# Gate and up projections of a SwiGLU in quads of 26 products instead of two units of 7

## The chip, the cores and the metric

One core of a Trainium2 chip runs the whole program. The metric is the device time of one execution in microseconds. The kernel has five instruction queues that matter here: PE (TensorE), DVE (VectorE), ACT (ScalarE), POOL (GpSimd) and SP, which only issues DMAs.

## The reference, cut to what matters

A two-layer decoder step for 512 prompt tokens and 8 x 4 sample tokens, so NT = 544 columns, all in float32. Layer 0 mixes tokens with sparse attention, layer 1 with a Mamba-2 scan; after each mixer comes

```python
x += swiglu(rms_norm(x, g), w_gate, w_up, w_down)

def swiglu(h, w_gate, w_up, w_down):                 # D_MODEL = 1024, FFN_HIDDEN = 2816
    return (jax.nn.silu(h @ w_gate) * (h @ w_up)) @ w_down
```

The change is in `h @ w_gate` and `h @ w_up` of both layers.

## The kernel before, in words

Activations lie transposed: 128 features on the partitions, 544 tokens in columns, cut in two halves n1 and n2 of 272. Every big projection is done by a fast matrix multiplication with 7 instead of 8 block products. A **unit** takes two weight tiles (128 outputs each), splits the inner dimension in two halves and the tokens in two halves, and so has 2x2 blocks of weights and 2x2 blocks of moving data. For gate and up an inner half is KH = 4 tiles of 128, so a product (`product`, L336) is 4 matmuls of 128x128 weights against 272 columns, added up in one PSUM bank. A float32 matmul stands in the trace as two records.

Around the products there are three kinds of sums. POOL forms four sums of weight blocks per unit (`weight_sums`, L391, each 128x512 for gate and up and 128x1408 for down); it may overwrite the sums of two units before only when PE has used them. DVE forms four sums of moving blocks once per stage (`moving_sums`, L407, each 128x1088). DVE and ACT then combine the seven products of a unit: ACT copies products 0 and 2 out of PSUM (`copy_product`, L360), DVE does seven additions of 272 columns (`sum_products`, L367), six of which read PSUM and one only SBUF (L387).

`swiglu` (L2199) runs, per layer, 22 gate and up units (unit 2k holds two gate tiles, unit 2k+1 the two up tiles of the same outputs) and then 4 down units, whose inner half is FH = 11 tiles. A gate or up tile is multiplied by rstd (the norm's factor, which is computed while the first units run) on DVE (L2313, L2316); ACT applies SiLU to the gate tiles (L2282); DVE multiplies gate and up (L2321) into `ffn_act`. When an upper tile of `ffn_act` is there, DVE at once makes its four sums for the down units (`act_turns`, L2294 to L2297).

The order on each queue is written out by hand and every instruction of ACT, DVE and POOL also waits for the one before it on its queue (`InOrder`). In the first gate and up units PE runs the four products that need no sums first (`EARLY`), then the norm's column sums (L497 strips, L505), then the rest. Weights come in slots of 1 MB through a ring of four (`ring_rounds`); SP refills a slot when PE signals `w_used`, for gate and up with the fourth product of every second unit. For the first down unit POOL's sums wait for all moving sums, and PE runs the first four products before it needs more than two of them:

```python
elif v == GU_UNITS and j >= 3:                                   # first down unit
    pe.wait_ge(f_sums, 4 * u + (2 if j == 3 else 4))
```

Of the kernel before, what the change touches and what calls it, by code (L numbers as in the profile page):

```python
# [19 lines left out]
P = 128  # L20
# [145 lines left out]

class InOrder:
# [13 lines left out]
def build(nc, t):  # L181
    ctx = ExitStack()
    with ctx:
# [102 lines left out]
        GU_UNITS, D_UNITS = FT, KT // 2  # L286
        U_NSA_IN, U_NSA_OUT, U_FFN, U_SSD_IN, U_SSD_OUT = 0, 10, (14, 64), 40, 60
        TURNS_BEFORE = {"nsa_in": 0, "nsa_out": 4, "ffn0": 8, "ssd_in": 12 + FH, "ssd_out": 16 + FH, "ffn1": 16 + 4 * KT + FH}
# [3 lines left out]


        unit_at, at = {}, 0
        for u in range(90):
            if u in (U_NSA_OUT, U_SSD_OUT):
# [4 lines left out]
            at += 9 if u in (U_NSA_IN, U_SSD_IN) + U_FFN else 7  # L301
# [3 lines left out]
        EARLY = [(0, 0), (0, 1), (1, 0), (1, 1)] + [(u, j) for u in range(2) for j in range(2, 7)]  # L305
        EARLY_SSD = [(0, 0), (1, 0), (0, 1), (1, 1)] + [(0, j) for j in (4, 6, 3, 5, 2)] + [(1, j) for j in range(2, 7)]
        early_at = {(u0 + u, j): n for u0, order in [(U_SSD_OUT, EARLY_SSD)] + [(u0, EARLY) for u0 in U_FFN]
                    for n, (u, j) in enumerate(order)}

        def pair_of(u):  # L310
            return max(u0 for u0 in (U_SSD_OUT,) + U_FFN if u0 <= u)

        def bank_of(u, j):
            if u < U_NSA_OUT:
                return (7 * u + j) % 6
            if (u, j) in early_at:
# [43 lines left out]
        def copy_product(act, do, u, j, dst):  # L360

            act.wait_ge(f_mm, multiplied(u, j))
            if u:
                act.wait_ge(f_added, 5 * (u - 1) + (2 if j == 0 else 5))
            do(act.activation(dst, bank_in(u, j), ACT.Copy), f_copied)  # L365

        def sum_products(dve, do, u, regs, c0, c1, after_u=None, between=lambda step: None):  # L367
# [4 lines left out]
            dve.wait_ge(f_copied, 2 * u + 1)  # L372
# [13 lines left out]
            dve.wait_ge(f_copied, 2 * u + 2)  # L386
# [182 lines left out]
        def p1_pe(pe):  # L569
# [48 lines left out]
            for u in range(10):  # L618
# [9 lines left out]
                for j, (a, b) in enumerate(operands(pair_slot(s), in_sums_of(u), (b11, b21, b22), in_t)):  # L628
# [13 lines left out]
                    if j >= 3:  # L642
                        pe.wait_ge(f_sums, 4 * u + {3: 2, 4: 2, 5: 3, 6: 4}[j])
# [1479 lines left out]
        def p5_pe(pe):  # L2123
            bank_user.clear()
            b11, _, b21, b22 = four_blocks(qT)
            for i in range(4):
                u, s = U_NSA_OUT + i, slot_at["nsa_out"] + i
                in_slot(pe, s)
                for j, (a, b) in enumerate(operands(pair_slot(s), out_sums[i % 2], (b11, b21, b22), out_t)):
# [4 lines left out]
                    if j >= 3:  # L2134
                        pe.wait_ge(f_sums, 4 * u + {3: 2, 4: 2, 5: 3, 6: 4}[j])
# [1376 lines left out]
```

## Time and profile before

| | us |
|---|---|
| median of 3 runs (lowest to highest) | 2271.1 (2264.6 to 2271.8) |
| span of the profiled execution, which is its own time here | 2268.8 |
| PE busy in it | 2153.3 |
| DVE busy | 1340.2 |
| POOL busy | 801.5 |
| ACT busy | 516.6 |

Times in the rows are microseconds from the span's start unless marked ns. "L346" is a line of the kernel, often a helper's; "sbuf<-sbuf,ps" says that an instruction writes SBUF and reads SBUF and PSUM; "xN" counts instructions (PE: records); "idle ... <-" says how long the engine stood idle before such instructions and what ended that. The chain of waits follows the work that ended last back to what released it. PEclk is the granted clock of TensorE as a share of full speed.

### The profile page before, as it was taken

What the parts mean: (1) busy time and instruction counts of PE and PEld (TensorE: products, weight loads), DVE (VectorE), ACT (ScalarE), POOL (GpSimd) and SP (SyncE); (2) the same over time, 40 slices, a digit from 0 to 9 for tenths busy, and PEclk for the clock granted to TensorE, in tenths of its full rate; (3) what the DMA queues carried; (4) which work ended last, traced back from release to release, by engine and by line L of the source; (5) the groups of instructions that cost most, each with busy time, mean ns of one, the idle gap of its engine ahead of it and who ended that gap; (6) DMA issues with size and microseconds to landing.
All of it is one profiled execution on the core that took longest, in us unless ns stands there. A gap on an engine that the chain in (4) does not pass through costs nothing.

```text
span 2268.8 us, 33739 instructions
## 1 busy us (share of the span) xinstructions
PE 2153.3 (95%) x11958; PEld 1703.1 (75%) x11958; DVE 1340.2 (59%) x2172; ACT 516.6 (23%) x1195; POOL 801.5 (35%) x702
## 2 busy tenths in 40 slices
PE   8999999998897679999999999999998999999999
PEld 6867777887675458888888878888556778888887
DVE  4456878764884125645652258876898445556422
ACT  2112112113685212111100023232563011111000
POOL 3321000001211742534325235554694533434242
PEclk8999999997899789999999999999999999999999
DMA  4134352313112962622112222222241221122212
GB/s 174 66 121 143 112 158 75 103 59 112 63 39 83 331 259 75 223 94 92 75 52 102 76 94 75 77 92 81 95 174 68 112 75 75 75 86 89 77 60 83
DMA packets 87735, 236.59 MB, mean 104 GB/s; under 512 B 11441, under 2 KB 60722, under 8 KB 73234
## 3 DMA queue, kind: packets, MB, share of 16 engines
q1 hardware_dynamic: 66722, 191.97, 23.7%
q0 software_dynamic: 7024, 29.90, 3.9%
q10 hardware_dynamic: 13824, 12.59, 1.8%
q8 instruction: 96, 1.57, 0.3%
q14 instruction: 69, 0.57, 0.1%
HBM read 217.95 MB, written 23.73 MB: 107 GB/s over the span
## 4 chain that ended last, share of the span: by engine, by line
PE 72%; DVE 15%; ACT 3%; issue 3%; SPq 3%; ACTq 1%; DMA 1%; POOL 1%; DVEq 0%; POOLq 0%
PE ps L346 57%; PE ps L1022 3%; PE ps L1538 2%; PE ps L1551 2%; PE ps L1571 1%; SPq L1861 1%; ACTq L862 1%; DVE sbuf L2577 1%; PE ps L935 1%; SPq L862 1%; ACT ps L3001 1%; DVE sbuf L1179 1%; DVE sbuf L1170 1%; DVE sbuf L1178 1%; DVE sbuf L1176 1%
## 5 line engine op out<-in xcount | busy, mean ns | idle before, releaser
L346 PE MATMUL ps<-sbuf 128*128 128x272 f32 x6048 | 1402.0, 394 | 19.2 <-DMA sbuf<-w_nsa_in 8.5
L346 PEld LDWEIGHTS ps<-sbuf 128*128 128x128 f32 x6048 | 1149.4, 191 | 269.5 <-issue 17.2
L396 POOL TENSOR_TENSOR sbuf<-sbuf 128x512 f32<-128x512 f32 (+2 forms) x90 | 135.7, 1508 | 710.1 <-PE ps L346 451.2
L365 ACT ACTIVATE sbuf<-ps 128x272 f32<-128x272 f32 x180 | 71.6, 398 | 1067.9 <-PE ps L346 1039.7
L1022 PE MATMUL ps<-sbuf 128*128 128x256 f32 (+1 forms) x1280 | 297.7, 392 | 5.5 <-ACT sbuf L1100 2.9
L1022 PEld LDWEIGHTS ps<-sbuf 128*128 128x128 f32 x1280 | 243.3, 191 | 58.5 <-issue 8.2
L376 DVE TENSOR_TENSOR sbuf<-sbuf,ps 128x272 f32<-128x272 f32 x90 | 39.4, 438 | 230.7 <-PE ps L346 229.6
L405 POOL TENSOR_TENSOR sbuf<-sbuf 128x512 f32<-128x512 f32 (+2 forms) x90 | 141.9, 1577 | 7.7 <-PE ps L346 0.9
L402 POOL TENSOR_TENSOR sbuf<-sbuf 128x512 f32<-128x512 f32 (+2 forms) x90 | 137.1, 1524 | 12.3 <-DVE sbuf L413 5.3
L397 POOL TENSOR_TENSOR sbuf<-sbuf 128x512 f32<-128x512 f32 (+2 forms) x90 | 134.6, 1496 | 7.1
L384 DVE TENSOR_TENSOR sbuf<-sbuf,ps 128x272 f32<-128x272 f32 x90 | 39.4, 438 | 123.5 <-PE ps L346 122.8
L379 DVE TENSOR_TENSOR sbuf<-sbuf,ps 128x272 f32<-128x272 f32 x90 | 39.3, 437 | 120.1 <-PE ps L346 119.1
L387 DVE TENSOR_TENSOR sbuf<-sbuf 128x272 f32<-128x272 f32 x90 | 103.3, 1148 | 3.1
L373 DVE TENSOR_TENSOR sbuf<-sbuf,ps 128x272 f32<-128x272 f32 x90 | 39.4, 438 | 85.6 <-PE ps L346 69.7
L1779 POOL MEMSET sbuf<- 128x512 f32 x1 | 0.5, 524 | 240.9 <-DVE sbuf L1231 240.9
L2316 DVE TENSOR_TENSOR sbuf<-sbuf 128x544 f32<-128x544 f32 x84 | 79.0, 940 | 2.9
L1726 DVE CUSTOM_DVE_ANT_0 sbuf<-ps,sbuf 128x128 f32<-128x128 f32 (+3 forms) x128 | 56.7, 488 | 32.0 <-PE ps L1538 25.1
L1630 ACT ACTIVATE sbuf<-sbuf 128x128 f32<-128x128 f32 (+3 forms) x128 | 70.6, 559 | 3.4 <-DVE sbuf L1726 3.3
L2577 DVE SCALAR_TENSOR_TENSOR sbuf<-sbuf 128x568 f32<-128x568 f32 x72 | 58.4, 811 | 19.3 <-ACT sbuf L2476 16.9
L389 DVE TENSOR_TENSOR sbuf<-sbuf,ps 128x272 f32<-128x272 f32 x90 | 39.3, 437 | 37.1 <-PE ps L346 34.7
L1861 POOL DMA_DIRECT2D sbuf<-sel_k x64 | 35.3, 552 | 65.3 <-ACTq L249 54.4
L1638 ACT ACTIVATE sbuf<-ps 128x128 f32<-128x128 f32 (+3 forms) x128 | 49.3, 434 | 38.0 <-PE ps L1551 37.2
(374 smaller groups left out, 2254.7 us busy)
## 6 DMA issues: line engine op xcount, KB each, us to landing
sbuf<-w_gu SPq DMA_DIRECT2D x44, 1024.0 KB, 4.9
sbuf<-w_down SPq DMA_DIRECT2D x32, 704.0 KB, 5.5
sbuf<-cmp_pages SPq DMA_DIRECT2D x160, 128.0 KB, 2.4
sbuf<-w_ssd_in SPq DMA_DIRECT2D x20, 1024.0 KB, 4.8
sbuf<-cmp_pages ACTq DMA_DIRECT2D x96, 128.0 KB, 3.1
sbuf<-w_nsa_in SPq DMA_DIRECT2D x9, 1024.0 KB, 4.8
sbuf<-sel_k SPq DMA_DIRECT2D x64, 128.0 KB, 2.5
sbuf<-sel_v SPq DMA_DIRECT2D x64, 128.0 KB, 5.1
```

Source lines behind the costliest of these rows:

```text
L346: last = pe.matmul(ps[:, bank_of(u, j), 0:HALF], a[:, kt * P:(kt + 1) * P], b[:, kt], start=kt == 0, stop=kt == kts - 1)
L365: do(act.activation(dst, bank_in(u, j), ACT.Copy), f_copied)
L387: do(dve.tensor_tensor(c1[:, n1], c1[:, n1], p4, ALU.add))
L396: do(pool.tensor_tensor(sv[:, 0], a21, a22, ALU.add), f_sums)
L397: do(pool.tensor_tensor(sv[:, 1], sv[:, 0], a11, ALU.subtract), f_sums)
L402: do(pool.tensor_tensor(sv[:, 2], a11, a21, ALU.subtract), f_sums)
L405: do(pool.tensor_tensor(sv[:, 3], a12, sv[:, 1], ALU.subtract), f_sums)
L1022: last = pe.matmul(product_of(u, j, ht), w[:, kt * 256 + ht * P:kt * 256 + (ht + 1) * P], moving[:, kt], start=kt == 0, stop=kt == KT - 1)
L1630: act.activation(S_, S_, ACT.Exp, scale=-1.0, bias=low[:, 0, s % 3, x:x + 1], accum_out=low[:, 1, s % 3, x:x + 1]).then_inc(a_exp, 1)
L1861: sp.dma_start(dst[:, i:i + 1], src[bass.ds(page, 1)].rearrange("o p n -> p o n")).then_inc(unit_in[place(kind, b)], 16)
L2316: do(dve.tensor_tensor(c[:, x], c[:, x], rstd, ALU.mult), g_took if v % 2 == 0 else None)
L2577: do(dve.scalar_tensor_tensor(acc[:, x], raw[:, x, k:k + CONV], conv_w[:, c, k:k + 1], acc[:, x], ALU.mult, ALU.add), r_conv if k == 3 els ...
```

## The change

Two units (two gate tiles, two up tiles, that is a gate unit and its up unit) become one **quad**: 4 weight tiles, the inner dimension in 4 quarters of KQ = 2 tiles, 2 token halves. It has 26 block products of 2 matmuls instead of 14 of 4. There are 11 quads a layer; the down units keep their 7 products.

- PE does the 26 products in a written order (`PRODUCTS`). Several products follow each other in one PSUM bank as a *chain*: PE goes on adding where the last product stood, but only when ACT (`COPIED`) or DVE (`SUMMED`) has read the value in between.
- POOL makes 28 sums of weight blocks a quad, each 128x256, in the order in which the products need them. They live in 13 places; a sum waits until the product that used its place is done. By the tables the 3rd sum is needed by the 3rd product, the 13th first by the 9th, the 28th by the last (26th). 15 sums of a layer's first quad find a place before any product; the 16th waits for product 3. POOL no longer waits for DVE's moving sums; it starts on them behind the sums of the output projection before.
- DVE makes 18 moving sums (*turns*) of 128x544 at the start of a layer's quads (11 of them before its first addition) instead of 4 of 128x1088. Per quad it does 19 additions of 272 columns, 15 of which read PSUM, then four products by rstd and, one quad later, two `gated` products, all 544 columns.
- ACT copies 9 values a quad (2 x 2 before) and does the two SiLUs of the quad before ahead of B1's copy.
- The moving sums of the down units are made in few long instructions: `lo` (11 tiles) in the 9th quad, `turn2` over 9 tiles in the 11th, and `turn4`, `turn3` and the last two tiles of each behind the last quad. POOL's sums for the first down unit wait for the last gated product.
- The two weight slots of a quad are released by its last product. out_win's store moves on POOL's queue from the 4th unit to the 2nd quad. ACT waits for two earlier stores, since buffers lie elsewhere.

```diff
+SUMMED = ("G1", "D3", "A1", "C1", "E2", "A2", "B3", "A3", "I1", None, "H2", "B4", "E4", "C3", "G2", "F4", None, None, None)
+        def quad_products(pe, n, block, place, raw, turned, before):
...
+            for i, p in enumerate(PRODUCTS):
+                a, b = FACTORS[p]
+                chain, k = IN_CHAIN[p]
+                bank = quad_banks[l][q][chain]
+                before(i)
...
+                else:
+                    name = chain + str(k)
+                    if name in COPIED:
+                        copied(pe, n, name)
+                    if name in SUMMED:
+                        summed(pe, n, SUMMED.index(name))
+                if isinstance(a, int):
+                    pe.wait_ge(f_sums, 4 * units_before(n) + len(SUMS) * n + SUMS.index(a) + 1)
...
+                for kt in range(KQ):
+                    last = pe.matmul(ps[:, bank, 0:HALF], weights[:, kt * P:(kt + 1) * P], moving[:, kt],
+                                     start=k == 0 and kt == 0, stop=kt == KQ - 1, skip_group_check=k > 0)
+                    if kt == 0 and i == len(PRODUCTS) - 1:
+                        last.then_inc(w_used, 2)
+                last.then_inc(f_mm, 1)
+        def quad_weight_sums(pool, do, n, block, place, waits):
...
+            for i, name in enumerate(SUMS):
+                x, op, y = BLOCK_SUMS[name]
+                if waits[i] > 0:
+                    pool.wait_ge(f_mm, products_before(units_before(n) - 1) + 7 + waits[i])
+                do(pool.tensor_tensor(place[i], place[SUMS.index(x)] if isinstance(x, int) else block(x),
+                                      place[SUMS.index(y)] if isinstance(y, int) else block(y), ops[op]), f_sums)
...
+                        if isinstance(b, int):
+                            pe.wait_ge(f_turns, TURNS_BEFORE[f"gu{l}"] + MOVING_ORDER.index(b) + 1)
+                        else:
+                            norm.wait_scaled(pe, KQ * int(b[0]) + KQ)
+                        if i == 5:
+                            norm.pe_strips(pe)
+                        if i == 8:
+                            norm.pe(pe)
...
+                def before_kt(v, j):
+                    def ready(kt):
+                        if j == 1:
+                            pe.wait_ge(prod, f0 + FH + kt + 1)
+                        elif j == 2 and kt in (0, READY):
+                            pe.wait_ge(f_turns, t0 + (2 if kt == 0 else 5))
...
+                for q in range(FFN_QUADS):
+                    c = quad_c[q % 2]
+                    quad_sums(dve, do, n0 + q, quad_regs, c, between(q))
+                    if q == 0:
+                        norm.invert(dve, do)
+                    for x in GATE_ROWS:
+                        do(dve.tensor_tensor(c[:, x], c[:, x], rstd, ALU.mult), g_took)
+                    for x in range(2):
+                        do(dve.tensor_tensor(c[:, x], c[:, x], rstd, ALU.mult))
+                turn4(slice(0, READY))
+                gated(FFN_QUADS - 1)
+                turn3(slice(0, READY))
+                turn2(LATER)
+                turn4(LATER)
+                turn3(LATER)
...
             def pool_part(pool):
+                if l == 0:
+                    pool.wait_ge(f_mm, multiplied(U_NSA_OUT, 0))
+                for q in range(FFN_QUADS):
+                    in_slot(pool, s0 + 2 * q)
+                    in_slot(pool, s0 + 2 * q + 1)
+                    quad_weight_sums(pool, pool_do, n0 + q, block_of(q), *places(q))
...
-                    if v == GU_UNITS:
-                        pool.wait_ge(f_turns, t0 + 4 + FH)
+                    if v == 0:
+                        pool.wait_ge(prod, f0 + FT)
+                    weight_sums(pool, pool_do, down_weights(v), down_sums, u0 + v - 1 if v else None)
```

## Rows read from the trace of the kernel before

**Rows 1.** The page, busy us of each engine (share of the span) and instructions

```profile
PE 2153.3 (95%) x11958; PEld 1703.1 (75%) x11958; DVE 1340.2 (59%) x2172; ACT 516.6 (23%) x1195; POOL 801.5 (35%) x702
```

**Rows 2.** Chain of waits, whole run: start us, length us, what

```profile
911.46 286.24 PE ps L346 x1248
...
1198.06 121.24 PE ps L346 x528
```

**Rows 3.** Busy by stretch: window, length, PE PEld DVE ACT POOL busy, PEclk, DMA, GB/s

```profile
911.40:1177.40 266.00, 265.94 (x1161) 220.54 (x1162) 157.20 (x244) 32.08 (x64) 102.58 (x80) 1.00 0.31 114
```

**Rows 4.** POOL by line in 911.5:1177: busy us, mean ns | idle before <-releasers

```profile
L397 POOL TENSOR_TENSOR sbuf<-sbuf 128x512 f32<-128x512 f32 x20 | 25.4, 1272 | 1.6
L396 POOL TENSOR_TENSOR sbuf<-sbuf 128x512 f32<-128x512 f32 x19 | 24.0, 1266 | 134.8 <-PE ps L346 126.9 <-DMA sbuf<-w_gu 7.9
```

**Rows 5.** POOL by line and shape, whole run

```profile
L396 POOL TENSOR_TENSOR sbuf<-sbuf 128x1408 f32<-128x1408 f32 x8 | 25.3, 3160 | 163.0 <-DVE sbuf L2297 62.6 <-DMA sbuf<-w_down 62.1 <-PE ps L346 38.3
...
L396 POOL TENSOR_TENSOR sbuf<-sbuf 128x1024 f32<-128x1024 f32 x4 | 9.4, 2354 | 52.2 <-DVE sbuf L3272 23.3 <-PE ps L346 21.7 <-DMA out_ssm_p<-sbuf 7.2
...
L3241 POOL TENSOR_TENSOR sbuf<-sbuf 32x256 f32<-32x256 f32 x4 | 3.2, 804 | 0.3
```

**Rows 6.** Timeline, POOL, 1009 to 1012.5: start us, length us, what

```profile
1009.90 1.27 POOL L402 TENSOR_TENSOR sbuf<-sbuf 128x512 f32<-128x512 f32 x1
1011.24 1.35 POOL L405 TENSOR_TENSOR sbuf<-sbuf 128x512 f32<-128x512 f32 x1
```

**Rows 7.** Timeline, DVE, 1009 to 1012.5

```profile
1009.91 1.55 DVE L387 TENSOR_TENSOR sbuf<-sbuf 128x272 f32<-128x272 f32 x1
```

**Rows 8.** DVE by line and shape, whole run

```profile
L376 DVE TENSOR_TENSOR sbuf<-sbuf,ps 128x272 f32<-128x272 f32 x90 | 39.4, 438 | 230.7 <-PE ps L346 229.6
...
L2321 DVE TENSOR_TENSOR sbuf<-sbuf 128x544 f32<-128x544 f32 x44 | 31.9, 725 | 1.5
...
L470 DVE RECIPROCAL sbuf<-sbuf 128x544 f32<-128x544 f32 x4 | 14.2, 3552 | 0.1
...
L2294 DVE TENSOR_TENSOR sbuf<-sbuf 128x272 f32<-128x272 f32 x22 | 9.7, 442 | 0.8
...
L412 DVE TENSOR_TENSOR sbuf<-sbuf 128x1088 f32<-128x1088 f32 x4 | 5.2, 1292 | 0.1
```

**Rows 9.** Timeline, POOL, 1209 to 1225

```profile
1216.59 3.52 POOL L402 TENSOR_TENSOR sbuf<-sbuf 128x1408 f32<-128x1408 f32 x1
```

**Rows 10.** Timeline, DVE, 1213 to 1225

```profile
1214.00 3.09 DVE L2306 TENSOR_TENSOR sbuf<-sbuf 128x544 f32<-128x544 f32 x1
1217.13 3.29 DVE L465 TENSOR_SCALAR sbuf<-sbuf 128x544 f32<-128x544 f32 x1
```

**Rows 11.** Chain of waits, 885 to 915

```profile
898.04 1.97 PE ps L497 x32
...
902.04 0.92 PE ps L505 x4
902.96 7.35 PE ps L346 x32
...
911.46 3.68 PE ps L346 x15
```

**Rows 12.** Timeline, DVE, 889 to 912

```profile
893.09 0.50 DVE L465 TENSOR_SCALAR sbuf<-sbuf 128x544 f32<-128x544 f32 x1
```

**Rows 13.** ACT by line and shape, whole run

```profile
L365 ACT ACTIVATE sbuf<-ps 128x272 f32<-128x272 f32 x180 | 71.6, 398 | 1067.9 <-PE ps L346 1039.7 <-DVE sbuf L376 16.3 <-DVE sbuf L389 7.9
L2282 ACT ACTIVATE sbuf<-sbuf 128x544 f32<-128x544 f32 x44 | 28.9, 657 | 6.7 <-DVE sbuf L2316 4.8
```

**Rows 14.** The page, DMA issues: count, KB each, median us from issue to landing

```profile
sbuf<-w_gu SPq DMA_DIRECT2D x44, 1024.0 KB, 4.9
sbuf<-w_down SPq DMA_DIRECT2D x32, 704.0 KB, 5.5
```

**Rows 15.** Timeline, POOL, 1180 to 1200

```profile
1194.81 3.15 POOL L405 TENSOR_TENSOR sbuf<-sbuf 128x1408 f32<-128x1408 f32 x1
```

More of the change, by code:

```diff
@@ new lines, with sums_in_order, need @@
+COPIED = ("D1", "H1", "F1", "D2", "F2", "B1", "E1", "B2", "C2")
+SUMMED = ("G1", "D3", "A1", "C1", "E2", "A2", "B3", "A3", "I1", None, "H2", "B4", "E4", "C3", "G2", "F4", None, None, None)
+MOVING_ORDER = (8, 15, 16, 20, 21, 10, 14, 12, 9, 22, 24, 11, 19, 13, 17, 18, 23, 25)
+def sums_in_order():
+    order = []
+    def need(n):
+        if isinstance(n, int) and n not in order:
+            need(BLOCK_SUMS[n][0])
+            need(BLOCK_SUMS[n][2])
+            order.append(n)
+    for p in PRODUCTS:
+        need(FACTORS[p][0])
+    return tuple(order)
@@ new lines, with sum_places @@
+SUMS = sums_in_order()
+PLACES = 13
+def sum_places(quads):
+    taken_by = {n: i for i, p in enumerate(PRODUCTS) for n in [FACTORS[p][0]]}
+    last_sum = {x: i for i, n in enumerate(SUMS) for x in BLOCK_SUMS[n]}
+    free, out = [(0, -1, -1)] * PLACES, []
+    for q in range(quads):
+        for i, n in enumerate(SUMS):
+            at = min((x for x in range(PLACES) if free[x][1] < q * len(SUMS) + i), key=lambda x: free[x][0])
+            out.append((at, free[at][0]))
+            by = len(PRODUCTS) * q + taken_by[n] + 1 if n in taken_by else free[at][0]
+            free[at] = (by, q * len(SUMS) + last_sum.get(n, -1), 0)
+    return out
@@ L2211, in weights @@
[L2211 to L2219 removed]
+            t0 = TURNS_BEFORE[f"down{l}"]
+            n0 = l * FFN_QUADS
@@ new lines, in between, with at_step @@
+                def between(q):
+                    def at_step(step):
+                        if q == 0 and step == 0:
+                            norm.take_strips(act, act_do)
+                        if q == 0 and step == 1:
+                            norm.root(act, act_do)
+                        if q and step == 2:
+                            silus(q - 1)
+                    return at_step
+                for q in range(FFN_QUADS):
+                    quad_copies(act, act_do, n0 + q, quad_regs, between(q))
@@ new lines, in between, with at_step @@
+                def between(q):
+                    def at_step(step):
+                        for name in TURNS_AT.get((q, step), ()):
+                            if name == MOVING_ORDER[15]:
+                                dve.wait_ge(n_ss, whole(norm.i))
+                            quad_turn(dve, do, name, raw, bc)
+                        if q and step == 2:
+                            gated(q - 1)
+                        if q == FFN_QUADS - 3 and step == 2:
+                            do(dve.tensor_tensor(lo[:, :, n2], lo[:, :, n2], lo[:, :, n1], ALU.subtract))
+                        if q == FFN_QUADS - 1 and step == 4:
+                            turn2(slice(0, READY))
+                    return at_step
```

413 lines of the change are left out of this document (260 added, 153 removed), and 16 rows, old and new, of tables (BLOCK_SUMS, FACTORS, TURN_SUMS).

## The prediction

> **What bounds the kernel now.** I read the page first, then the chain of waits, then the busy time of one stretch, then POOL and DVE line by line in it. The page shows PE busy 95% of the span [rows 1], and the chain shows how: in each layer's gate, up and down stage it is one unbroken run of L346 matmuls, 1248 records in 286.24 us and 528 in 121.24 us, which is 0.2294 and 0.2296 us a record [rows 2]. A matmul is two records, so the first kind of run holds products of 8 records and the second products of 22, at the same pace: the start of a product, with its waits, costs PE nothing visible, and halving products should cost nothing there. Between 911.4 and 1177.4 PE is busy 265.94 of 266.00 us, at a granted clock of 1.00, so 2.4 GHz; POOL is busy 102.58 us there [rows 3], and its idle time is almost all spent waiting for PE to free the places of its weight sums, 126.9 of 134.8 us in front of L396 [rows 4]. So PE is the bound and POOL has slack, which the change spends.
>
> **PE: what goes.** Two units are 14 products of 8 records, 112 x 0.2294 = 25.69 us. A quad is 26 products of 4 records, 104 x 0.2294 = 23.86 us. That is 1.83 us a quad, 20.2 us for 11 quads, 40.4 us for two layers.
>
> **POOL: what comes.** A quad needs 28 sums of 128x256 in place of 8 of 128x512. The trace has no 128x256 sum. The nearest rows lie on a line: 1.27 us for 512 columns [rows 4], 2.35 for 1024 and 3.16 for 1408 [rows 5], so 2.11 ns a column and a constant 0.18; that gives 0.72 at 256. Bounds: half of the 512 sum, 0.63, from below, and the 0.80 us of the 32x256 product of L3241 [rows 5] from above; I take the line's 0.72. One sum starts 0.08 us after the end of the one before (1009.90 + 1.27 to 1011.24) [rows 6]. 28 x 0.80 = 22.4 us of a 23.86 us quad, where two units used 8 x 1.35 = 10.8.
>
> On top come DVE instructions that read two operands from SBUF. L387 takes 1.55 us when it meets a POOL sum [rows 7] and the same shape takes 0.44 where POOL is idle [rows 8]: it ends 0.3 us after the sum that it met, and the next sum takes 1.35 instead of 1.27 [rows 6], 0.08 to 0.09 more. After a 544-column one the POOL sum takes 3.52 [rows 9] instead of 3.16: 0.36 more, half of DVE's own 0.725 [rows 8]. Nor do they pass each other: L2306 and L465 each sit out a whole sum, 3.09 and 3.29 us [rows 10]. A quad has four such instructions of 272 columns (three ends of sums and n35 + F2) and six of 544 (four by rstd, two gated), so POOL loses 4 x 0.09 + 6 x 0.36 = 2.5 us: 24.9 us a quad. DVE itself has room: 15 PSUM reads at 0.44 plus ten instructions that each wait for at most one sum come to some 17 us.
>
> The Trainium skill ("SBUF — State Buffer", section "Who interferes with whom") says that VectorE and GpSimd share a pair of SBUF ports under an exclusive lock, and that the loser stays blocked for the whole instruction of the winner. On the waiting side the rows agree (3.09 us); on POOL's side they show half the instruction, 0.36 of 0.725. By the rule POOL would lose 4 x 0.44 + 6 x 0.725 = 6.1 us a quad, and a quad would take 28.5 us; by the rows 24.9. I take the rows.
>
> So POOL, not PE, sets the pace in the long run, by 24.9 - 23.86 = 1.05 us a quad. It starts ahead: 15 sums find a place before the first product, while PE is still in the output projection. The tight spot is the 9th product, which is first to need the 13th sum. After product 3 POOL works freely through sums 16 to 28 (13 x 0.89, that is 24.9 / 28 each, to 14.3 us into quad 1) and the first 13 of quad 2 (to 25.9 us); the 9th product of quad 2 comes at 23.86 + 8 x 0.917 = 31.2: 5.3 us ahead. Quad 1 changes that little: PE also does the norm's 2.9 us [rows 11] and some stalls, and POOL meets 18 turns at 0.36. I take 4 us of lead, gone after four quads; the last six run at POOL's pace: 6 x 1.05 = **+6.3 us** a layer.
>
> Two long DVE turns hold POOL up for longer: 11 tiles (2992 columns) in quad 9 and 9 tiles (2448) in quad 11. On the line of 0.44, 0.725 and 1.29 us [rows 8] they take 3.27 and 2.71 us; POOL loses all but 0.36 of each: **+5.2 us** (bounds: 1, if POOL has slack then and only PE's wait for DVE is left, and 6.0).
>
> **The start.** Before, PE ran its four early products, strips (1.97 us), norm (0.92) and lost 1.15 us between 902.96 + 7.35 and 911.46 [rows 11]. Now the first three products need six scaled tiles; the 4th needs the eighth, at 893.59 [rows 12], about when it comes. The 6th needs the second turn, at 0.76 us a turn alone or 1.16 behind sums, so 0.8 us late; the 22nd needs the 17th turn, 0.6 us late: **+0.3 us** net (bounds -1 and 3). ACT's two new waits are for stores that are over: POOL waited for out_ssm_p ahead of its first output-projection sum [rows 5], and the first copy comes behind a whole product after that. The store of out_win leaves POOL's queue about a quad later; nothing on the path reads it.
>
> **Quad 2.** DVE finishes quad 1 (4.3 us), inverts (3.55 [rows 8]) and scales two gate tiles (2.3); then ACT, in order, does two SiLUs (0.66 each) ahead of B1's copy (0.40) [rows 13]: at about 12.6 us with hand-overs, for a product due at 13 x 0.917 = 11.9: **+1.0 us** (0 to 2). In later quads the invert is gone and the copy is in time by some 0.5 us. Weights, now released by a quad's last product, still land in time: two loads of 4.9 us [rows 14], needed 11 us later.
>
> **The down stage's start.** Before, POOL's four sums for the first down unit ended at 1194.81 + 3.15 = 1197.96 [rows 15], when PE had just done that unit's first four products (the run of [rows 2] ends at 1197.70), and the fifth started 0.4 us late, at 1198.06. Now, from the end of the last quad: nine DVE additions (to 3.2 us), four by rstd (6.2), the t4 turn of nine tiles (9.0), two gated (10.5), and only then may POOL begin its four sums of 3.16, while DVE's t3 turn of nine tiles and three turns of two tiles remain. By [rows 9, 10] they alternate. If POOL comes first, its sums end at 13.8, 19.4, 23.0 and 26.6 and the turn that the third product's tenth step needs at 23.6; dense, that step is at 14.2, so the fifth product starts 9.5 us late. If DVE comes first the turn is there at 20.7 and the fourth sum at 27.0, against 20.2: 6.9 us late. The hand-over to POOL and DVE's next start are equally quick, so I take the middle less the old 0.4: **+7.8 us** (bounds 3.0, without any alternation, and 9.1). The stage's last two weight slots come free with the last product and are filled by then (5.5 us each [rows 14]).
>
> **Sum.** Per layer -20.2 + 6.3 + 5.2 + 0.3 + 1.0 + 7.8 = +0.4 us, +0.8 in two: 2269.6 for the profiled execution's 2268.8, and 2271.9 beside the median of 2271.1, which lies 2.3 above that span. What gates it is one number: POOL's waits are about 10 x the shortfall per quad - 4, so each 0.01 us in a POOL sum is 2.8 us a layer, 5.6 in all.
>
> **Rivals.**
> - *POOL keeps up.* A 256-column sum at 0.63 to 0.69 us: 28 x 0.71 + 2.5 = 22.4, below PE's 23.86. Then 6.3 goes, 5.2 becomes 1: -10 a layer, 2251. If the alternation is also milder (down start 3.0), -15.9 a layer: 2239. For: POOL's slack now is 60%. Against: the line of three shapes.
> - *POOL slower still* (the other side). At L3241's 0.80 us a quad costs POOL 27.1: shortfall 3.3, 29 us a layer of waiting in every quad from the third on at the 9th product: +23 a layer, 2318. It decides from 0.73 us a sum (+0.3%). For: the constant part may be larger with a wait in front of nearly every sum. Against: L402 has such a wait and 0.08 us in front of it.
> - *A DVE instruction holds POOL up for its whole length* (4 x 0.44 + 6 x 0.725). 28.5 us a quad, 42 us of waiting a layer: +37 a layer, 2346. The 0.36 us speaks against it. This is what the rule of the Trainium skill above would make of it.
> - *The change gives PE nothing:* products of 4 records cost 0.07 us more each, which eats 1.83 us a quad: about 2312. The equal paces in rows 2 speak against it.
>
> **How the numbers follow.** Forecast case 0.48 (0.10 of it faster by over 0.3%, 0.26 within 0.3%, 0.12 slower; 0.3%, 6.8 us, is what a measurement of this kernel can tell from no change). POOL keeps up 0.28, POOL slower 0.16, whole-instruction blocking 0.03, nothing for PE 0.05. Faster 0.10 + 0.28 = 0.38, same 0.26, slower 0.12 + 0.24 = 0.36. The likeliest case alone spans 2258 to 2290 (sum at 0.70 to 0.74, either order at the down start). The range leaves out the milder alternation below and most of the three slow cases above: 2245 to 2305.
>
> **What would show it.** PE's gate and up stretch: 26 x 4 records a quad at 0.229 us. POOL's 128x256 sums at 0.72 us, nearly back to back in quads 6 to 11, with 1.1 us after a 544-column DVE instruction. PE waiting for a POOL sum at one place in late quads, about 1 us, and hardly in quads 3 and 4. A hole of 7 to 9 us between products 3 and 5 of each down stage. I am wrong if POOL still idles on PE in the late quads, if PE waits for DVE or ACT inside ordinary quads, or if the down stage starts densely.

## The result, and the profile after

The changed kernel takes 2288.45 us (median of 4 runs, 2286.14 to 2290.73), beside 2269.0 for the kernel before on the same chip (4 runs): a ratio of 1.0077, 95% interval 1.006 to 1.0093. It is 0.8% slower. The ratios here and below are formed from the fast runs alone (one execution of experiment 1, which took 6117 us, is left out) and differ by up to 0.1% from the quotient of two medians, here 1.0086. The forecast was 2272, 0.8 us over the kernel before, with a range of 2245 to 2305. The profiled execution has a span of 2286.3 us, 17.5 longer than before.

The page answers to [rows 1]; below its first line stand two groups of its fifth part (line, engine, operation, shapes, count, busy us, mean ns, idle before and what ended it). L598 is the sum of weight blocks, L585 the matmul of a quad.

```profile
PE 2128.6 (93%) x11782; PEld 1668.7 (73%) x11782; DVE 1431.2 (63%) x2236; ACT 560.2 (25%) x1305; POOL 1104.7 (48%) x1142
...
L598 POOL TENSOR_TENSOR sbuf<-sbuf 128x256 f32<-128x256 f32 x616 | 523.6, 850 | 84.5 <-PE ps L585 27.5
L585 PE MATMUL ps<-sbuf 128*128 128x272 f32 x2288 | 534.5, 394 | 29.5 <-POOL sbuf L598 24.5
```

PE is busy 24.7 us less and the span is 17.5 us longer: PE has new idle time. The second group says where 24.5 us of it is, in front of quad matmuls and behind POOL's sums. (That PE's busy time fell by 24.7 us and not by the forecast's 40.4 is no contradiction: a record is counted as 0.39 us long and the next one starts 0.23 us after it, so every new stop, and every record at half clock, adds busy time. The pace shows below.) POOL has 303 us more work.

The busy time of layer 1's quads by stretch, one row a quad, answers to [rows 3] (window, length, busy PE PEld DVE ACT POOL, granted clock, DMA share, GB/s). The rows left out are quads 4, 5 and 7, which repeat their neighbours (23.83, 23.83 and 25.08 us).

```profile
1850.72:1879.31 28.59, 27.84 (x142) 20.87 (x141) 26.50 (x36) 6.23 (x13) 22.63 (x23) 1.00 0.00 1
1879.31:1904.28 24.97, 24.10 (x106) 19.67 (x105) 19.11 (x26) 6.17 (x12) 22.77 (x29) 1.00 0.22 85
1904.28:1928.11 23.83, 23.83 (x105) 19.75 (x104) 15.97 (x26) 4.89 (x11) 21.79 (x27) 1.00 0.24 89
...
1975.77:2000.61 24.84, 24.08 (x105) 19.68 (x104) 15.63 (x25) 4.89 (x11) 22.64 (x29) 1.00 0.22 86
...
2025.69:2050.78 25.09, 24.07 (x105) 19.68 (x104) 15.84 (x26) 4.89 (x11) 22.89 (x29) 1.00 0.22 84
2050.78:2078.58 27.80, 24.79 (x105) 19.43 (x104) 19.53 (x27) 4.89 (x11) 25.67 (x28) 1.00 0.21 76
2078.58:2103.88 25.30, 24.12 (x105) 19.59 (x104) 16.05 (x26) 4.89 (x11) 23.04 (x29) 1.00 0.22 84
2103.88:2131.11 27.23, 24.31 (x105) 19.59 (x104) 19.08 (x28) 4.89 (x11) 22.12 (x24) 1.00 0.14 54
```

Counting quads from 1: the third to fifth run at PE's pace, 23.83 us. In the sixth POOL's lead runs out, and from then on a quad takes 25.1. The POOL column, with 0.08 us after each of 28 sums (2.2 us), fills it: 22.89 + 2.2 = 25.1. PE's waits between 1904 and 2131 us (what waited for what, us in total, times, longest) have one cause only:

```profile
PE ps L585 <- POOL sbuf L598: 9.9, 10, 1.9
```

Quads 9 and 11, with the long DVE turns, take 27.80 and 27.23. The eleven take 280.40 us, where 22 units took 287.07 from their first record to the first down product.

Layer 0's eleven quads take 288.66. Their third and fourth are the ones that differ:

```profile
944.79:970.38 25.59, 24.00 (x105) 19.59 (x104) 17.60 (x30) 4.89 (x11) 16.70 (x20) 1.00 0.91 314
970.38:999.44 29.06, 25.34 (x104) 19.35 (x105) 14.34 (x23) 4.89 (x11) 26.41 (x33) 1.00 0.16 67
```

In the third the DMA engines are 91% busy and POOL works for 16.70 us only. POOL's timeline from 935 to 975 us (start, length, what, idle before and its releaser) shows why:

```profile
937.42 0.55 POOL L2635 DMA_DIRECT2D out_win<-win  x1 [0.30 <-POOL sbuf L598]
937.98 25.00 POOL L598 TENSOR_TENSOR sbuf<-sbuf 128x256 f32<-128x256 f32 x28
970.51 5.07 POOL L598 TENSOR_TENSOR sbuf<-sbuf 128x256 f32<-128x256 f32 x5 [7.53 <-DMA sbuf<-w_gu]
```

and the DMA view of 930 to 1000 us says how long the transfers took (issuing queue, count, KB each, median us to landing); the last line is from the view of w_gu in 935 to 1000 us, the same six loads:

```profile
sbuf<-w_gu SPq DMA_DIRECT2D x6, 1024.0 KB, 7.0
out_win<-win POOLq DMA_DIRECT2D x1, 28.6
...
DMA to landing us min/median/max: 4.6/7.0/25.0
```

POOL issues out_win's store at 937.42. It takes 28.6 us to land, and the weight loads share the DMA engines with it: the slowest of the six took 25.0 us. POOL stands still for 7.53 us, and its lead does not cover that: PE pays 1.76 us in the third quad, 5.23 in the fourth and 1.01 in the fifth (24.84). The same stop is in the kernel before, in the very row that the prediction read for POOL's slack: the second releaser of L396, 7.9 us for w_gu [rows 4]. There PE did not wait at all between 912 and 1000 us.

At the down stage, PE's, POOL's and DVE's timelines in layer 0 answer to [rows 9, 10 and 15]:

```profile
1179.90 9.33 PE L462 MATMUL ps<-sbuf 128*128 128x272 f32 x40
1189.72 5.61 PE L462 MATMUL ps<-sbuf 128*128 128x272 f32 x22 [0.49 <-DVE sbuf L2572]
1200.40 9.94 PE L462 MATMUL ps<-sbuf 128*128 128x272 f32 x36 [5.07 <-DVE sbuf L2581]
```

```profile
1190.60 5.58 POOL L512 TENSOR_TENSOR sbuf<-sbuf 128x1408 f32<-128x1408 f32 x1 [14.00 <-DVE sbuf L2572]
1196.26 3.51 POOL L513 TENSOR_TENSOR sbuf<-sbuf 128x1408 f32<-128x1408 f32 x1
1199.85 3.51 POOL L518 TENSOR_TENSOR sbuf<-sbuf 128x1408 f32<-128x1408 f32 x1
1203.44 3.53 POOL L521 TENSOR_TENSOR sbuf<-sbuf 128x1408 f32<-128x1408 f32 x1
```

```profile
1190.46 2.71 DVE L2584 TENSOR_TENSOR sbuf<-sbuf 128x2448 f32<-128x2448 f32 x1
1193.20 3.56 DVE L2578 TENSOR_TENSOR sbuf<-sbuf 128x544 f32<-128x544 f32 x1
1196.80 3.55 DVE L2581 TENSOR_TENSOR sbuf<-sbuf 128x544 f32<-128x544 f32 x1
```

DVE came first with its t3 turn (L2584), POOL's first sum had to sit it out (5.58 us for a sum of 3.16), and then DVE's two-tile turns sat out whole POOL sums. The turn that the third product needs (L2581) ends at 1200.35, 20.45 us after the last quad; POOL's fourth sum ends 27.07 after it. The prediction's "DVE first" order had 20.7 and 27.0.

Where the 17.5 us are: quads of layer 0 +1.6, of layer 1 -6.7; first down units +8.1 and +8.6 (43.96 and 44.50 us for 35.89); Mamba output projection +3.8 (110.8 for 107.0); attention and all the rest +2.1. (The quads' and units' lengths are the distances between the starts of their first matmuls.)

### The profile page after: what moved, and what is told of

Same layout as the page of the kernel before. It is cut to its first block, busy times and chain, and to the rows that moved or that the text cites. A ratio compares the mean times of both kernels' runs of the same rounds, so it can differ in the third digit from the quotient of the medians.

```text
span 2286.3 us, 35024 instructions
## 1 busy us (share of the span) xinstructions
PE 2128.6 (93%) x11782; PEld 1668.7 (73%) x11782; DVE 1431.2 (63%) x2236; ACT 560.2 (25%) x1305; POOL 1104.7 (48%) x1142
## 4 chain that ended last, share of the span: by engine, by line
PE 62%; DVE 18%; POOL 8%; issue 4%; SPq 3%; ACT 3%; ACTq 1%; DMA 1%; POOLq 0%; DVEq 0%
PE ps L462 31%; PE ps L585 14%; POOL sbuf L598 8%; PE ps L1259 4%; PE ps L1775 2%; PE ps L1788 2%; PE ps L1808 1%; SPq L2098 1%; DVE sbuf L604 1%; PE ps L1172 1%; DVE sbuf L2874 1%; SPq L1099 1%; PE ps L1663 1%; ACTq L1099 1%; DVE sbuf L1416 1%
## 5 line engine op out<-in xcount | busy, mean ns | idle before, releaser
L462 PE MATMUL ps<-sbuf 128*128 128x272 f32 x3584 | 844.0, 397 | 30.2 <-DVE sbuf L2581 10.1
L462 PEld LDWEIGHTS ps<-sbuf 128*128 128x128 f32 x3584 | 682.3, 192 | 189.4 <-issue 15.7
L598 POOL TENSOR_TENSOR sbuf<-sbuf 128x256 f32<-128x256 f32 x616 | 523.6, 850 | 84.5 <-PE ps L585 27.5
L585 PE MATMUL ps<-sbuf 128*128 128x272 f32 x2288 | 534.5, 394 | 29.5 <-POOL sbuf L598 24.5
L585 PEld LDWEIGHTS ps<-sbuf 128*128 128x128 f32 x2288 | 431.1, 190 | 132.3 <-issue 30.0
L1259 PEld LDWEIGHTS ps<-sbuf 128*128 128x128 f32 x1280 | 245.0, 193 | 59.9 <-issue 6.9
L512 POOL TENSOR_TENSOR sbuf<-sbuf 128x512 f32<-128x512 f32 (+2 forms) x46 | 84.6, 1838 | 345.7 <-PE ps L462 207.1
L481 ACT ACTIVATE sbuf<-ps 128x272 f32<-128x272 f32 x92 | 36.6, 398 | 626.9 <-PE ps L462 589.9
L614 ACT ACTIVATE sbuf<-ps 128x272 f32<-128x272 f32 x198 | 78.7, 397 | 427.4 <-PE ps L585 264.6
L492 DVE TENSOR_TENSOR sbuf<-sbuf,ps 128x272 f32<-128x272 f32 x46 | 20.1, 438 | 117.6 <-PE ps L462 116.8
L518 POOL TENSOR_TENSOR sbuf<-sbuf 128x512 f32<-128x512 f32 (+2 forms) x46 | 81.8, 1779 | 8.8 <-DVE sbuf L529 5.3
L521 POOL TENSOR_TENSOR sbuf<-sbuf 128x512 f32<-128x512 f32 (+2 forms) x46 | 83.4, 1814 | 4.4 <-PE ps L462 1.0
L513 POOL TENSOR_TENSOR sbuf<-sbuf 128x512 f32<-128x512 f32 (+2 forms) x46 | 79.6, 1730 | 3.6
L495 DVE TENSOR_TENSOR sbuf<-sbuf,ps 128x272 f32<-128x272 f32 x46 | 20.1, 437 | 72.8 <-PE ps L462 72.2
L500 DVE TENSOR_TENSOR sbuf<-sbuf,ps 128x272 f32<-128x272 f32 x46 | 20.1, 438 | 66.4 <-PE ps L462 65.7
L489 DVE TENSOR_TENSOR sbuf<-sbuf,ps 128x272 f32<-128x272 f32 x46 | 20.2, 438 | 63.7 <-PE ps L462 48.5
```

Of the source, the lines that this page charges most:

```text
L462: last = pe.matmul(ps[:, bank_of(u, j), 0:HALF], a[:, kt * P:(kt + 1) * P], b[:, kt], start=kt == 0, stop=kt == kts - 1)
L512: do(pool.tensor_tensor(sv[:, 0], a21, a22, ALU.add), f_sums)
L513: do(pool.tensor_tensor(sv[:, 1], sv[:, 0], a11, ALU.subtract), f_sums)
L518: do(pool.tensor_tensor(sv[:, 2], a11, a21, ALU.subtract), f_sums)
L521: do(pool.tensor_tensor(sv[:, 3], a12, sv[:, 1], ALU.subtract), f_sums)
L585: last = pe.matmul(ps[:, bank, 0:HALF], weights[:, kt * P:(kt + 1) * P], moving[:, kt], start=k == 0 and kt == 0, stop=kt == KQ - 1, skip_ ...
```

## The experiments

Each starts from the changed kernel. Ratios are to the kernel before, timed on the same chip: 2271.95 us beside the first four, 2271.67 beside the last three.

**1. win_late: is it the store?** POOL issues out_win's store only after its last sum of the Mamba input projection and DVE's last addition there, at 1592.6 us, long after layer 0's quads.

```diff
-                    if l == 0 and q == 1:
-                        pool.dma_start(t["out_win"], t["win"]).then_inc(stored, 16)
...
+            pool.wait_ge(stored, 32)
+            pool.dma_start(t["out_win"], t["win"]).then_inc(stored, 16)
...
-            pool.wait_ge(stored, 48)
+            pool.wait_ge(stored, 32)
```

> The changed kernel with one thing moved: the out_win store is issued from POOL after the SSD input projection instead of after the sums of the second quad of layer 0. Theory A (the store's transfer, 28.6 us from 937.4, slows the two weight loads that land in the same time, POOL stands 7.5 us for the slot of quad 4, and PE follows): layer 0's quads 3 and 4 go from 25.6 and 29.1 us to 23.8 each as in layer 1, layer 0's gate and up stretch from 288.7 to about 280.4, the kernel 8 us faster, near 2280. Rival B (layer 0's weights are late for another reason, such as the ring still filling after the output projection): quads 3 and 4 stay at 25 to 29 us, no change in time.

Measured: 2278.38 us (median of seven), ratio 1.0023 (1.0001 to 1.0045). Layer 0's third and fourth quads, by stretch:

```profile
940.58:964.41 23.83, 23.83 (x105) 19.76 (x104) 15.98 (x27) 4.89 (x11) 21.79 (x27) 1.00 0.24 89
964.41:988.24 23.83, 23.83 (x105) 19.76 (x104) 15.75 (x25) 4.89 (x11) 21.75 (x27) 1.00 0.23 88
```

Both are at PE's pace, the DMA share fell from 0.91 to 0.24, and the store still takes 28.5 us where it is now; no engine is seen to wait for it there. It was the store: 1.76 + 5.23 us in these two quads and 1.01 in the fifth, which takes 23.83. The eleven gain 6.2 (282.46), not 8.0, above all because the last quad took 28.95 instead of 27.23: the granted clock of that stretch was 0.94 (last section).

**2. down_order: is the late turn what costs at the down start?** The turns of the last two tiles go ahead of the t3 turn.

```diff
-                turn3(slice(0, READY))
                 turn2(LATER)
                 turn4(LATER)
+                turn3(slice(0, READY))
                 turn3(LATER)
...
-                            pe.wait_ge(f_turns, t0 + (2 if kt == 0 else 5))
+                            pe.wait_ge(f_turns, t0 + (2 if kt == 0 else 4))
```

> The changed kernel with the last DVE turns in another order: turn2 and turn4 of the last two tiles come right behind the last gated product, ahead of turn3 over nine tiles. Theory A (POOL's four 3.2 us sums and DVE's turns alternate on a shared resource, so whatever comes first, the fourth sum is there about 27 us after the last quad): the hole of 9 us inside the third down product goes, but a hole of nearly the same size appears before the fifth product, which starts at 26 to 27.5 us instead of 28; gain 1 to 4 us over both layers. Rival B (the hole is only the turn's lateness): the fifth product starts near 21 us, gain 6 us or more a layer, 12 to 14 us in all.

Measured: 2285.66, ratio 1.0066 (1.0043 to 1.0089). PE's and POOL's timelines at the same place:

```profile
1190.50 6.53 PE L462 MATMUL ps<-sbuf 128*128 128x272 f32 x26 [0.47 <-DVE sbuf L2572]
1198.63 5.31 PE L462 MATMUL ps<-sbuf 128*128 128x272 f32 x22 [1.60 <-POOL sbuf L513]
1207.85 14.47 PE L462 MATMUL ps<-sbuf 128*128 128x272 f32 x55 [3.92 <-issue]
```

```profile
1198.65 5.51 POOL L518 TENSOR_TENSOR sbuf<-sbuf 128x1408 f32<-128x1408 f32 x1
1204.24 3.51 POOL L521 TENSOR_TENSOR sbuf<-sbuf 128x1408 f32<-128x1408 f32 x1
```

The stop of 5.07 us became one of 1.60 and one of 3.92. The second is labelled "issue", yet it ends 0.10 us after POOL's last sum (1204.24 + 3.51 = 1207.75): what ended it has to be read from the other engine's timeline. The t3 turn now meets POOL's third sum instead of its first, and the fourth sum ends 27.06 us after the last quad, as theory A has it. Rival B, with the fifth product near 21 us, falls. The first down unit takes 44.84 us, no less than before the edit: its fifth product starts 0.8 us earlier (27.16 us after the last quad for 27.98), but behind the 3.92 us stop, at a granted clock of 0.59 over the next 4 us, it takes 6.74 us where 5.04 is the dense length. So the 1 to 4 us of theory A are not there in the profile. One of two waits was removed, and the other took its place.

**3. down_split: down_order, and the fifth product waits for two sums instead of four.**

```diff
-                            pe.wait_ge(f_sums, sums_before(u) + (2 if j == 3 else 4))
+                            pe.wait_ge(f_sums, sums_before(u) + (2 if j < 5 else 4))
...
-                        if j == (4 if v == 0 else 3):
+                        if j == (5 if v == 0 else 3):
```

> As the kernel with the reordered turns, and PE's fifth product of the first down unit waits for two weight sums instead of four (it needs the first only); the four slots are released by the sixth product instead of the fifth. Theory A (what is late is POOL's third and fourth sum, at 20 to 27 us): products 1 to 5 run with holes of 2 us at most, the sixth starts near 28 us instead of 33, the unit takes 38 to 39 us instead of 44; 10 to 12 us faster than the changed kernel, near 2277. Rival B (the slots released later than before make the second down unit wait for its weights): the unit is as short, but 4 to 6 us come back in the second unit.

Measured: 2272.16, ratio 0.9999 (0.9988 to 1.0011). PE's timeline:

```profile
1191.02 6.53 PE L462 MATMUL ps<-sbuf 128*128 128x272 f32 x26 [0.48 <-DVE sbuf L2572]
1199.15 20.43 PE L462 MATMUL ps<-sbuf 128*128 128x272 f32 x88 [1.60 <-POOL sbuf L513]
```

One stop of 1.60 us is left, and 88 records follow it densely. The first down unit takes 39.06 us in both layers, 4.9 and 5.4 less than in the changed kernel, and the second takes 35.37 as before, so rival B falls. The profiled span fell by 12.2 us. Outside these two gains the Mamba output projection took 107.1 us instead of 110.8, which the edit does not touch, and layer 1's last quad 1.7 us more, at half clock. The median fell by 16 us, more than theory A's 10 to 12; what lies beyond the 10.3 does not show in the part that was edited.

**4. drop2: is POOL's pace the bound?** Sums 39 and 42 are not made.

```diff
-    ... 39: ("21", "-", "11"), ... 42: ("22", "-", "02"), ...
-    ... 5: (39, 22), ... 24: (42, 25), ...
+    ... 5: ("21", 22), ... 24: ("22", 25), ...
```

> The changed kernel without two of POOL's 28 sums a quad (39 and 42): their products read a raw weight block instead, so the result of gate and up is another one; PE, DVE and ACT do the same work. Theory A (late quads run at POOL's pace, 28 sums at 0.80 us plus 2.5 us lost to DVE instructions with two SBUF operands): POOL needs 23.5 us a quad, less than PE's 23.86, so quads 6 to 8 go from 25.1 to 23.9, quads 9 and 11 lose the most of their 2 to 4 us, gate and up of layer 1 goes from 280.4 to about 270, the kernel is 17 to 20 us faster. Rival B (late quads are paced by DVE, whose additions come late behind blocked instructions, or by PE's own product starts): quads 6 to 8 stay at 25.1 us, no change.

Measured: 2261.71, ratio 0.9948 (0.993 to 0.9965). A middle quad of layer 1 by stretch:

```profile
1986.43:2010.26 23.83, 23.83 (x105) 19.76 (x104) 15.98 (x26) 4.89 (x11) 21.25 (x27) 1.00 0.23 88
```

Quads 3 to 8 and 10, 11 of layer 1 all take 23.83 us, quad 9 24.97. Layer 1's eleven fell by 11.3 us to 269.11, as theory A has it, 2.83 of it in quad 9 and 3.40 in quad 11, where POOL now pays for most of the long turns itself. Rival B falls. The kernel gained more than the 17 to 20 us expected, 24.8 in the profiled span and 27 in the median: layer 0's quads fell by 14.6, since POOL's lead now also pays for part of the stop behind the store (1.76 us in its third quad, 1.01 in its fifth; the fourth stays at 29.10).

**5. norstd: is part of POOL's pace what DVE takes from it?** The four 544-column multiplications by rstd are left out; POOL keeps all 28 sums.

```diff
-                    for x in GATE_ROWS:
-                        do(dve.tensor_tensor(c[:, x], c[:, x], rstd, ALU.mult), g_took)
-                    for x in range(2):
-                        do(dve.tensor_tensor(c[:, x], c[:, x], rstd, ALU.mult))
...
-                        act.wait_ge(g_took, f0 + 2 * q + x + 1)
+                        summed(act, n0 + q, len(SUMMED) - 1)
```

> Left out: the four 544-column multiplications by rstd on VectorE in each quad (gate and up come out unscaled). GpSimd keeps all of its sums. Theory A (the two engines take turns: while one of these multiplications runs, the POOL sum beside it takes 1.09 us in place of 0.725): four such sums of each quad get 0.36 us back, POOL's pace in quads 5 to 7 falls from 25.1 to 25.1 - 4 x 0.36 = 23.65 us, under PE's 23.83, so these quads take 23.83 to 23.9; layer 1's eleven quads go from 280.4 to 271 to 277, and the time from 2287 to 2270-2280. Rival B (POOL's pace is its own sums and what is between them, VectorE costs it nothing): quads 5 to 7 stay at 25.1 and the time at 2284-2290. Rival C (VectorE holds POOL back for its whole instruction, 1.13 us each): pace 25.1 - 4.5 = 20.6, the quads at 23.83 all the same, but POOL idle for over 2 us of each quad.

Measured: 2260.35, ratio 0.994 (0.9916 to 0.9963); layer 1's quads 269.40 us. POOL by line in quads 6 to 8 of layer 1, first of the changed kernel, then of this one:

```profile
L598 POOL TENSOR_TENSOR sbuf<-sbuf 128x256 f32<-128x256 f32 x85 | 69.4, 817 | 6.7
```

```profile
L598 POOL TENSOR_TENSOR sbuf<-sbuf 128x256 f32<-128x256 f32 x85 | 64.5, 758 | 7.8 <-PE ps L585 1.9
```

The same sums take 4.9 us less in three quads, 1.6 us a quad for four multiplications, 0.41 each (0.36 expected), and POOL waits for PE again. Theory A's mechanism holds; rival B, with no effect of DVE, and rival C, with 4.5 us a quad, do not. Theory A's ranges, 271 to 277 us and 2270 to 2280, were missed on the fast side: quads 9 and 11 fell by 2.6 and 3.4 us, and the first down units, with four multiplications fewer ahead of them, by 3.0 and 4.3.

**6. dve_sums: two of POOL's sums on DVE.**

```diff
+DVE_SUMS = {39: ("21", "11"), 42: ("22", "02")}
...
+                def weight_sum(q, n):
...
+                    do(dve.tensor_tensor(dve_place[n], block_of(q)(x), block_of(q)(y), ALU.subtract), dve_sum)
```

> Two of the 28 sums of each quad (39 and 42) go from GpSimd to VectorE, which has two additions of 256 columns more, at the start of the quad and after its fifth step. Theory A (POOL's pace was the bound, VectorE has 9 us of 25 free): POOL's pace falls by 2 x 0.82 us and gets back at most 2 x 0.25 in turns lost to the new additions, 25.1 - 1.6 + 0.5 = 24.0 at most, 23.6 at least; quads 5 to 7 take 23.83 to 24.0 in both layers, layer 1's eleven quads 269 to 274 (280.4 before), layer 0's 274 to 281 with the stop behind out_win's store still in it, and the time is 2262 to 2272. Rival B (VectorE becomes the bound: its chain of reads of the banks stands behind the new additions, and PE waits for VectorE where it waited for POOL): quads at 25 us and over, no gain or a loss, 2285 to 2300.

Measured: 2263.17, ratio 0.9964 (0.9944 to 0.9983); quads 274.60 and 271.53 us. Theory A's numbers hold, and rival B's do not. The price is at the start: quads 1 and 2 of layer 1 take 29.95 and 25.93 us instead of 28.59 and 24.97. There PE waits for DVE, which has two additions more, and in quad 2 for an ACT copy that comes behind DVE's work (1.9 us instead of 0.9).

**7. all_four: experiments 1, 2, 3 and 6 together.**

> Four edits together: out_win's store behind the last GpSimd sum of the program's state-space part, the turns of unit 0's last rows ahead of its third turn, the down unit's fifth product waiting for two sums only, and sums 39 and 42 on VectorE. If the parts are what they seem: two waits around the down start give 4.9 to 5.4 us in each layer plus the slow records behind them (in all 11 to 15), the store 6 to 8, the POOL pace 16 to 25, from 2287: 2240 to 2254, 0.7 to 1.4% under the kernel before. Rival: the gains overlap (the long turns of quads 8 and 10 fall on VectorE, which has two additions more) and it comes out at 2258 to 2268, within 0.5% of the kernel before.

Measured: 2247.04, ratio 0.9883 (0.9861 to 0.9905): 1.2% under the kernel before, and 1.9% under the changed one by the two ratios (0.9883 / 1.0077). The eleven quads of either layer, then both down stages:

```profile
891.50:1163.07 271.57, 266.88 (x1181) 218.31 (x1180) 210.81 (x311) 57.71 (x125) 231.99 (x271) 1.00 0.21 79
1826.70:2098.24 271.54, 267.18 (x1181) 218.11 (x1180) 210.25 (x311) 56.42 (x124) 232.09 (x271) 1.00 0.20 76
1163.07:1307.86 144.79, 141.98 (x617) 116.52 (x615) 60.57 (x57) 8.43 (x16) 55.46 (x16) 1.00 0.26 99
2098.24:2243.03 144.79, 141.99 (x617) 116.52 (x615) 52.73 (x51) 4.49 (x10) 55.55 (x16) 1.00 0.22 82
```

Quads are 17.1 and 8.9 us shorter than in the changed kernel, down stages 4.9 and 5.4: 36.3 of the span's 38.3. One by one the edits took 39.5 us out of the same parts: 6.2 the store (layer 0's quads), 14.1 and 8.9 the sums on DVE, 4.9 and 5.4 the down start. The 3.2 that are missing are in layer 0's quads (17.1 for 6.2 + 14.1): the sums on DVE alone had already paid for part of the store's stop. So the gains add up but for that, and the rival's 2258 to 2268 falls.

## Why the prediction was right, and where it was not

The time lies in the stated range, but the range is 60 us wide, and within it the forecast was no change: +0.8 us, with 0.38 for faster, 0.26 for the same and 0.36 for slower. The span grew by 17.5. Layer 1 came nearly as worked out, +1.9 us for +0.4. Layer 0 has +9.7 for +0.4, 8.3 of it from the store, and 5.9 lie outside the changed part, where the forecast had nothing. So the account of POOL and of the waits at the down start was right and the total was too low; that the time still fell in the range is due to its width.

Layer 1 can be checked term by term. The 22 units before are 11 pairs, of which ten take 25.67 us each and the first, with the norm in it, 30.40.

| step | predicted, us | layer 1, us | from |
|---|---|---|---|
| PE's matmuls | -20.2 | -20.2 | 11 x (23.83 - 25.67) |
| start | +0.3 | 0.0 | quad 1's excess over 23.83 (4.76) less the first pair's over 25.67 (4.73) |
| quad 2 | +1.0 | +1.1 | 24.97 - 23.83 |
| POOL's pace and long turns | +6.3 + 5.2 | +12.4 | quads 6 to 11 over 23.83 |
| down start | +7.8 | +8.6 | 44.50 - 35.89 |
| sum | +0.4 | +1.9 | |

**POOL's sum and its pace: right.** The step that gated the result was the price of a shape that the trace did not have. The line through 512, 1024 and 1408 columns gave 0.72 us; POOL's timeline, taken where DVE leaves it alone and where DVE multiplies by rstd, has

```profile
1992.35 0.72 POOL L598 TENSOR_TENSOR sbuf<-sbuf 128x256 f32<-128x256 f32 x1
...
2005.55 1.09 POOL L598 TENSOR_TENSOR sbuf<-sbuf 128x256 f32<-128x256 f32 x1
```

that is 0.72 and 0.72 + 0.37, as worked out from [rows 4 to 10]. A quad takes POOL 25.1 us (24.9 predicted), the last six quads are the long ones, and PE waits for POOL ten times in them, 9.9 us in all. "POOL keeps up" and "POOL slower still" fall with this number, and the equal paces of [rows 2] held too, so "the change gives PE nothing" falls. Experiments 4 and 6 show that it is POOL's pace, and experiment 5 that the DVE instructions are the second part of it. (One of the first rival's sums is off: 0.4 - 6.3 - 4.2 - 4.8 is -14.9 a layer and not -15.9, which makes 2241 of its 2239.)

**Whole-instruction blocking: the block is there, its price was too high.** The Trainium skill ("SBUF — State Buffer", section "Who interferes with whom") has it that whichever of the two starts second waits for the other's whole instruction. The trace agrees: whatever the length of the DVE instruction, a POOL sum that meets it ends 0.58 or 0.59 us after it (last section). The prediction's rival took this as a loss of DVE's whole length, 0.44 us for 272 columns and 0.725 for 544; measured are 0.09 and 0.37, so the rival falls. But the prediction's reading of the rows, half of the instruction, is right for 544 columns only: POOL loses DVE's length less 0.35 to 0.36. In quads 9 and 11 the longest sums take 3.64 and 3.07 us, 2.92 and 2.35 over 0.72, for turns of 3.27 (the prediction's line) and 2.71 (as L2584 above), as the prediction's "all but 0.36 of each" had it.

**The down start: right in its waits, in size partly by luck.** The hole is at the third product, where the turn is late. The prediction left open which engine would come first, called POOL's hand-over and DVE's next start equally quick, and took the middle of two orders, 7.8. They are not equally quick: in layer 0 DVE started 0.03 us after the last gated product, which ended at 1190.43, and POOL 0.17 after it, and in layer 1 DVE came first as well. For that order the prediction had 6.9 less 0.4, 6.5; 8.1 and 8.6 were measured. The difference is two things that it did not foresee. By the sums alone the fifth product would start at 27.1 us after the last quad; it starts at 27.98 and 28.52, since PE came out of the hole at half its clock (below). The other 0.7 us is a wait for DVE's L505 at the end of the unit, which stays in experiments 3 and 7; its cause was not followed up. Experiment 2 showed both waits of the prediction to be real.

**The failed step: the store.** The prediction says of out_win's store that it leaves POOL's queue about a quad later and that "nothing on the path reads it", and so puts it at nothing in the sum. That is true of its data, and beside the point: the store occupies the DMA engines that bring the next weights. The 7.9 us stop stood in [rows 4] as the smaller of two releasers. It cost nothing as long as POOL had slack, and the change spends that slack; all 7.5 us came through, 8.3 in layer 0's quads with POOL's lead gone earlier. Experiment 1 shows it.

**Outside the changed part.** The Mamba output projection takes 110.8 us, 107.0 before. It has a stop of PE behind DVE that is 1.8 us long in the kernel before, 2.75 here and 2.5 in down_order. After the 2.75 us stop PE ran eight records at half clock; after the shorter ones it did not, and the whole stretch takes 107 us. The code there is the same but for one more wait of ACT, for an earlier store, and the place of POOL's sums. Six of the eight kernels with quads show about 110.5, all after a stop of 2.75 to 3.05 us, and two about 107. What decides it stays open, and with it some 4 us of the difference. The rest's +2.1 us is less than what varies by itself: the first quad starts at 886.8 to 896.8 us in the eight kernels, whose edits all act later.

## What to carry to other kernels

When a change spends an engine's slack, every stop that the slack used to pay for comes due: list all releasers of that engine's idle time, the small ones too, and charge each one anew. Price a missing shape by a line through its nearest shapes, and multiply by the count before deciding which engine is the bound; here 1.6 us less of POOL's work a quad, 0.06 us for each of 28 sums, was the difference between 0.8% slower and 0.5% faster (experiment 4). Before removing a wait, look for one that stands hidden behind it: removing the first alone turned a stop of 5.07 us into one of 1.60 and one of 3.92, and only experiment 3, which removed both, made the unit shorter.

## What the runs showed of the hardware

Three things were not expected.

A DVE instruction that reads two SBUF operands and a POOL sum hold each other up, and the one that waits has about 0.14 us of its own work behind it when the other ends. DVE's and POOL's timelines in quads 7 and 9 of layer 1 show it at three lengths:

```profile
2003.16 0.85 DVE L663 TENSOR_TENSOR sbuf<-sbuf 128x272 f32<-128x272 f32 x1
2004.92 1.13 DVE L2609 TENSOR_TENSOR sbuf<-sbuf 128x544 f32<-128x544 f32 x1
2064.59 3.68 DVE L2598 TENSOR_TENSOR sbuf<-sbuf 128x2992 f32<-128x2992 f32 x1
```

```profile
2003.78 0.81 POOL L598 TENSOR_TENSOR sbuf<-sbuf 128x256 f32<-128x256 f32 x1
2004.67 0.80 POOL L598 TENSOR_TENSOR sbuf<-sbuf 128x256 f32<-128x256 f32 x1
2065.21 3.64 POOL L598 TENSOR_TENSOR sbuf<-sbuf 128x256 f32<-128x256 f32 x1
```

The first DVE instruction ends at 2004.01 and the POOL sum beside it at 2004.59; the second at 2006.05 and its sum (2005.55 + 1.09, shown above) at 2006.64; the third at 2068.27 and its sum at 2068.85. Each time POOL ends 0.58 or 0.59 us later, 0.14 less than the 0.72 of a sum alone, and so do 237 of the run's 243 quad sums that take 0.78 us or more. The other way round, the second DVE instruction ends 0.58 us after the POOL sum before it (2005.47), 0.14 less than its own 0.725. A POOL sum begins 0.08 us after the one before it, so where the two take turns POOL loses DVE's own length less 0.14 + 0.08 + 0.14 = 0.36. Measured are 0.09 of 0.44 us, 0.37 of 0.725, 2.35 of 2.71 and 2.92 of 3.27 (the last length from the prediction's line), 0.35 to 0.36 less each time. The 1408-column sum at the down start, which had no sum before it and began 0.14 us after the turn, lost 2.42 of 2.71.

A stop of PE can be followed by half clock. After the 5.07 us hole of the first down unit, the busy time by stretch is

```profile
1194.00:1200.40 6.40, 1.33 (x6) 0.76 (x4) 6.33 (x3) 0.00 (x0) 6.24 (x3) 0.96 0.00 0
1200.40:1204.40 4.00, 4.00 (x11) 3.14 (x12) 3.96 (x2) 0.40 (x1) 3.92 (x2) 0.64 0.00 0
1204.40:1208.40 4.00, 4.00 (x19) 3.29 (x19) 0.26 (x2) 0.00 (x0) 2.57 (x1) 1.00 0.00 0
```

with a granted clock of 0.64 in the four microseconds after it: records come every 0.45 us, the level of 1.2 GHz, and then every 0.23, that of 2.4. The hole costs more than its length: 26 records after its end, at 20.50 us, the fifth product would start at 20.50 + 26 x 0.229 = 26.46 us after the last quad and starts at 27.98, 1.5 us later (2.1 in layer 1). After down_split's stop of 1.60 us the records come every 0.23 at once, but the length of the stop alone does not decide it. In norstd the two layers have the same stop of 3.09 us at the down start, and the 4 us after it are

```profile
1190.20:1194.20 4.00, 4.00 (x11) 3.15 (x12) 3.97 (x2) 0.40 (x1) 3.92 (x2) 0.62 0.00 0
2126.93:2130.93 4.00, 4.00 (x18) 3.33 (x18) 3.97 (x2) 0.40 (x1) 3.92 (x2) 1.00 0.00 0
```

And layer 0's last quad has a wait of 1.90 us for POOL in win_late, after which 24 records took 7.43 us, and one of 1.89 in the changed kernel, after which they took 5.74. What else decides it was not found.

The store that POOL issues took 28.0 to 28.6 us to land wherever it stood, and beside it 1 MB loads of another queue, with a median of 4.9 us [rows 14], took as much as 25.0.
